# Moving the rounded operands of a float32r block kernel to other byte places in SBUF

## What is computed

```python
h = rms_norm(x, norm_pre_w)
proj = jnp.einsum('bsd,df->bsf', h, w_in)              # 1024 -> 10256
qkv_a, z_a, beta_a, dec_a, qkv_b, z_b, gate_logits = jnp.split(proj, cuts, axis=-1)
qkv_a = silu(causal_depthwise_conv(qkv_a, conv_w))      # then l2_normalize of q and k
oa = gated_delta_rule(qa, ka, va, g, beta)              # chunks of 64, 8 heads
ya = rms_norm(oa, dn_onorm_w) * silu(z_a)
ob = moba_attention(qb, kb, vb, rel_bias)
yb = ob * silu(z_b)
merged = gates[:, :, 0] * (ya @ w_branch[0]) + gates[:, :, 1] * (yb @ w_branch[1])
out = x + rms_norm(merged @ w_out, norm_post_w)
```

## Time and profile before

| | |
|---|---|
| median of 3 runs | 357.52 us (357.3 to 357.66) |
| the profiled execution | 357.55 us |
| its span, first to last instruction | 355.8 us |
| PE busy | 347.6 us, 98% |
| PEld (weight loads) busy | 318.4 us, 89% |
| DVE, ACT, POOL busy | 270.0, 218.8, 58.7 us |
| granted TensorE clock, mean | 0.998 |

### The profile page before, as it was taken

The page is one execution under the profiler, slowest core; times in us unless marked ns, Lnnn a source line. Parts: engine busy times, 40 slices in busy tenths (PEclk is TensorE's granted clock), DMA queues, the critical chain, the costliest instruction groups (busy, mean ns, idle before and its releaser), DMA issues.

```text
span 355.8 us, 6674 instructions
## 1 busy us (share of the span) xinstructions
PE 347.6 (98%) x2387; PEld 318.4 (89%) x2387; DVE 270.0 (76%) x551; ACT 218.8 (62%) x483; POOL 58.7 (16%) x114
## 2 busy tenths in 40 slices
PE   7999999999999999999999999999999999999993
PEld 5889998888899999999999999999998888888882
DVE  3869897599997868978788797878977656566744
ACT  5877894542457667686867766777676544425421
POOL 1534436500050000301103020030301101000011
PEclk9999999999999999999999999999999999999999
DMA  8667948793698485446745565465534735766423
GB/s 264 178 193 194 334 158 270 198 329 119 167 257 228 121 214 141 121 122 164 188 120 128 145 178 147 120 164 145 165 121 138 247 118 172 254 226 236 124 113 118
DMA packets 76206, 63.48 MB, mean 178 GB/s; under 512 B 4724, under 2 KB 62478, under 8 KB 76174
## 3 DMA queue, kind: packets, MB, share of 16 engines
q1 hardware_dynamic: 73838, 59.37, 57.3%
q0 software_dynamic: 1152, 3.30, 3.1%
q10 hardware_dynamic: 1184, 0.39, 0.5%
HBM read 61.46 MB, written 1.59 MB: 177 GB/s over the span
## 4 chain that ended last, share of the span: by engine, by line
PE 84%; DVE 8%; DMA 3%; issue 2%; ACT 1%; POOL 0%; DVEq 0%; SPq 0%; ACTq 0%; POOLq 0%
PE banks L1395 40%; PE banks L1450 15%; PE banks L1657 6%; PE banks L1413 6%; DVE w_lo L919 3%; DVE sub L1061 2%; DMA xin<-in_x_dram 1%; DMA raw<-in_w_in_dram 1%; DMA sub<-m_blocks 1%; PE banks L1545 1%; PE banks L1523 1%; PE banks L1562 1%; PE banks L1551 1%; PE banks L1380 1%; DVE sub L1063 1%
## 5 line engine op out<-in xcount | busy, mean ns | idle before, releaser
L919 DVE TENSOR_TENSOR w_lo<-raw,w_hi 128x1024 fp32r<-128x1024 f32 x102 | 123.8, 1220 | 42.3 <-ACT w_hi L670 41.6
L670 ACT CAST w_hi<-raw 128x1024 fp32r<-128x1024 f32 x103 | 107.2, 1047 | 30.0 <-PE banks L1450 12.3
L1395 PE MATMUL banks<-h_hi,w_hi 128*128 128x256 f32 x440 | 64.0, 288 | 0.2 <-DVE acc L989 0.2
L1395 PE MATMUL banks<-h_lo,w_hi 128*128 128x256 f32 x440 | 59.4, 277 | 0.0
L1395 PE MATMUL banks<-h_hi,w_lo 128*128 128x256 f32 x440 | 59.3, 277 | 0.0
L1395 PEld LDWEIGHTS banks<-h_hi,w_hi 128*128 128x128 f32 x440 | 55.2, 189 | 0.7 <-DVE acc L989 0.3
L1395 PEld LDWEIGHTS banks<-h_hi,w_lo 128*128 128x128 f32 x440 | 54.2, 188 | 0.0
L1395 PEld LDWEIGHTS banks<-h_lo,w_hi 128*128 128x128 f32 x440 | 54.2, 188 | 0.0
L989 DVE SCALAR_TENSOR_TENSOR acc<-banks,vec,acc 128x255 f32<-128x255 f32 (+2 forms) x72 | 34.5, 480 | 3.7 <-ACT acc L790 1.5
L616 POOL TENSOR_TENSOR so<-so,rnq 128x2 f32<-128x2 f32 x8 | 2.0, 251 | 162.8 <-ACT junk L857 162.8
L790 ACT ACTIVATE acc<-banks,vec 128x256 f32<-128x256 f32 x16 | 7.6, 473 | 17.4 <-PE banks L1395 17.4
(11 more groups left out here) (258 smaller groups left out, 607.6 us busy)
## 6 DMA issues: line engine op xcount, KB each, us to landing
raw<-in_w_in_dram SPq DMA_DIRECT2D x80, 512.0 KB, 4.9
raw<-in_w_branch_dram SPq DMA_DIRECT2D x16, 512.0 KB, 4.7
raw<-in_w_out_dram SPq DMA_DIRECT2D x8, 512.0 KB, 4.2
xin<-in_x_dram SPq DMA_DIRECT2D x2, 512.0 KB, 3.8
th_E<-g_rows POOLq DMA_DIRECT2D x2, 512.0 KB, 7.2
bias<-bias_rows POOLq DMA_DIRECT2D x1, 1024.0 KB, 7.5
raw<-in_x_dram SPq DMA_DIRECT2D x2, 512.0 KB, 3.7
out_dram<-xin SPq DMA_DIRECT2D x4, 256.0 KB, 2.0
```

The lines of the kernel that those rows point to most:

```text
L670: nc.scalar.copy(w_hi[:, t % SLOTS, :], raw[:, t % SLOTS, :]).then_inc(s_hi, 1)
L919: v.tensor_tensor(w_lo[:, t % SLOTS, cols], raw[:, t % SLOTS, cols], w_hi[:, t % SLOTS, cols].bitcast(F32), ALU.subtract).then_inc(s_lo, 1)
L1395: last = mm(ps, w, r, start=part == 0 and k == 0, stop=part == 2 and k == KT - 1)
```

## The change

The declarations are put in another order. No instruction is added, removed or moved on any engine; operands have other addresses. Six small tensors, 1,984 bytes in all, now stand ahead of `raw`, three more and `h`, `y` follow the weights, and `xin` and the rest come after these.

| tensor | byte before | mod 2048 | mod 256 | byte after | mod 2048 | mod 256 |
|---|---|---|---|---|---|---|
| `raw` | 16512 | 128 | 128 | 18496 | 64 | 64 |
| `w_hi` | 32896 | 128 | 128 | 34880 | 64 | 64 |
| `w_lo` | 49280 | 128 | 128 | 51264 | 64 | 64 |
| `h_hi` | 77632 | 1856 | 64 | 67840 | 256 | 0 |
| `h_lo` | 85824 | 1856 | 64 | 76032 | 256 | 0 |
| `y_hi` | 193088 | 576 | 64 | 84224 | 256 | 0 |
| `y_lo` | 209472 | 576 | 64 | 100608 | 256 | 0 |
| `wbd2` | 76416 | 640 | 128 | 17280 | 896 | 128 |
| `xin` | 65664 | 128 | 128 | 116992 | 256 | 0 |
| `kT_all` | 108992 | 448 | 192 | 141824 | 512 | 0 |
| `act` | 121280 | 448 | 192 | 154112 | 512 | 0 |
| `bT` | 125376 | 448 | 192 | 158208 | 512 | 0 |
| `pt` | 189504 | 1088 | 64 | 222272 | 1088 | 64 |
| `vtok_all` | 161216 | 1472 | 192 | 194048 | 1536 | 0 |

Slices start at whole multiples of 512 bytes (128 columns), 1024 bytes (256 columns) or 2048 bytes (512 columns) behind the start of their tensor.

```diff
+        gt = sb("gt", [P, 12, NC, HEADS])
+        wbd2 = sb("wbd2", [P, KT, 4 * HEADS], F32R)
+        ssqk = sb("ssqk", [P, NC, HEADS])
+        ng = sb("ng", [P, NC, HEADS])
+        so = sb("so", [P, 8])
+        mx = sb("mx", [P, 8])
         raw = sb("raw", [P, SLOTS, D])
         w_hi = sb("w_hi", [P, SLOTS, D], F32R)
         w_lo = sb("w_lo", [P, SLOTS, D], F32R)
+        bd = sb("bd", [P, NC, 2 * HEADS])
+        alog = sb("alog", [P, HEADS])
+        dtb = sb("dtb", [P, HEADS])
+        h_hi = sb("h_hi", [P, KT, SEQ], F32R)
+        h_lo = sb("h_lo", [P, KT, SEQ], F32R)
+        y_hi = sb("y_hi", [P, 2, HEADS, SEQ], F32R)
+        y_lo = sb("y_lo", [P, 2, HEADS, SEQ], F32R)
         xin = sb("xin", [P, NC, D])
...
         wbd = sb("wbd", [P, KT, 2 * HEADS])
-        wbd2 = sb("wbd2", [P, KT, 4 * HEADS], F32R)
         bd_lo = sb("bd_lo", [P, NC, 2 * HEADS])
-        alog = sb("alog", [P, HEADS])
-        dtb = sb("dtb", [P, HEADS])
-        h_hi = sb("h_hi", [P, KT, SEQ], F32R)
-        h_lo = sb("h_lo", [P, KT, SEQ], F32R)
...
-        y_hi = sb("y_hi", [P, 2, HEADS, SEQ], F32R)
-        y_lo = sb("y_lo", [P, 2, HEADS, SEQ], F32R)
```

More of the change, by code:

```diff
@@ L140, in build @@
         wbd = sb("wbd", [P, KT, 2 * HEADS])
-        wbd2 = sb("wbd2", [P, KT, 4 * HEADS], F32R)
         bd_lo = sb("bd_lo", [P, NC, 2 * HEADS])
-        alog = sb("alog", [P, HEADS])
-        dtb = sb("dtb", [P, HEADS])
-        h_hi = sb("h_hi", [P, KT, SEQ], F32R)
-        h_lo = sb("h_lo", [P, KT, SEQ], F32R)
         bias = sb("bias", [P, HEADS, SEQ])
         tiny = sb("tiny", [P, 32])
-        bd = sb("bd", [P, NC, 2 * HEADS])
-        gt = sb("gt", [P, 12, NC, HEADS])
         tab = sb("tab", [P, 11, HEADS])
-        ng = sb("ng", [P, NC, HEADS])
         grow = sb("grow", [HEADS, SEQ])
-        ssqk = sb("ssqk", [P, NC, HEADS])
         tk = sb("tk", [P, 2, NC, HEADS])
@@ L178, in build @@
         junk = sb("junk", [P, 512])
-        so = sb("so", [P, 8])
         lac = sb("lac", [P, 2, 2, P])
         sc = sb("sc", [P, BIAS_W])
-        mx = sb("mx", [P, 8])
         pt = sb("pt", [P, BIAS_W])
         y32 = sb("y32", [P, 2, SEQ])
-        y_hi = sb("y_hi", [P, 2, HEADS, SEQ], F32R)
-        y_lo = sb("y_lo", [P, 2, HEADS, SEQ], F32R)
         m0 = sub[:, 0:D]
```

## The result

The changed kernel takes 359.64 us (median of 4, 359.44 to 360.07) where the kernel before takes 357.54: a ratio of 1.0061, 95% interval 1.0044 to 1.0079. It is slower by 2.1 us. The forecast was "no visible effect", 357.5 us; the range held the time, the direction was wrong.

What follows compares the result with a forecast made beforehand. PE was taken as the bound, at full clock. All terms were 0, so the span stayed 355.8 + 0 us and the median forecast was 357.5 us, no visible effect (chance 0.42); range 353.5 to 360.0 us.

Steps and rivals of the forecast that it cites:

- What bounds the kernel: PE, busy 347.6 of 355.8 us and 84% of the chain; four lines with rounded operands alone are 67%.
- Step (a) and (b): Rounded matmuls on PE: new places of the weights (`raw`, `w`) and of `h`, `y` change their time by 0.
- Step (c): All other tensors moving, including `xin`, the VectorE `w_lo` step and float32 matmuls: 0, with 0.2 us either side before PE.
- Float32 matmuls of the heads: Float32 matmuls on PE, whose operands also move: 0, because row pairs at different places took equal time.
- Rival 3: L1395's 1320 weight loads at odd multiples of 64 bytes make PE wait; mostly 358.3 to 360 us; chance 0.24.
- rival 2: Rounded matmuls at L1395 and the 512-column lines lose much of their surplus; 347.8 to 355 us; chance 0.12.
- Rival 1: 512-column lines run faster with moving weights at `h`'s old place modulo 256; 1.0 us, giving 356.5 us; chance 0.22.
- Rival 4: Whole kernel: the declarations don't set the tensors' places; would give 357.5 us as well; no separate chance.
- The terms beside PE: First transfer `xin`, 4.34 us, and VectorE's `w_lo` step, 1218 ns each: 0 with 0.2 us on either side.

Runs made afterwards that it cites:

- `all_shift`: The kernel before with every tensor moved together by 1984 bytes, all distances between tensors kept; 357.45 us, ratio 0.9993.
- `cst_act_place`: The kernel before with `cst` and `act`, both operands of the transposes L1537 and L1540, at the change's distances from `h` and `w`; 358.04 us, ratio 1.0019.
- `rest_place`: The changed kernel with `w`, `h` and `y` put back to their old places modulo 256, everything else as in the change; 359.43 us, ratio 1.0048.

## Why the prediction was wrong

**What bounds the kernel** held: PE was the bound, and what the stretches lost, 2.2 us, came through in the span, which grew by 2.4.

**Step (a) and (b), the places of `w` and `h`: 0.** Right, and for the reason given last: the distance is unchanged. `all_shift` gave `w`, `h` and `y` the change's places modulo 256 and moved all others with them: 0.9993. But the reason given first, that no pair of rows sees its place, was wrong. The rows compared operands at one distance modulo 256 only; the same places at another distance cost 6 us. That the distance modulo 512 doesn't count was right (229.0 against 229.2 ns at 64 and 320, and at L1395 the fast rate at 320 before and at 64 in `cst_act_place`). So was it that crossing 2 KB costs nothing: every second slice of `h` crosses, and the single starts go 113, 113, 114 by turns of three.

**Step (c), everything else: 0.** This is the step that failed: "Float32 matmuls of the heads: 0". `rest_place`, in which only the other tensors differ from before modulo 256, has 25 slow stretches and 359.43 us. I asked whether a moved float32 matmul would itself take longer, and it does not: L1545 to L1552 take what they took. I did not ask what it does to the rounded stretch behind it. The row for this stood in the trace: two rates for identical stretches, 2.74 and 2.83 us. I used it as a price and left open what chooses between them. Two of 46 were slow, and the other 44 were fast because of places that the change did not keep. By what mechanism those places act on the stretch behind stays open.

**Rival 3** had the direction and, per matmul, the price: 3.8 ns. Its cause was wrong. Weight loads at an odd multiple of 64 bytes cost nothing (`all_shift`), and "all of them at that rate" became 24 more stretches, 576 matmuls, 2.2 us. Its sign, L1395 above 115 ns with the 512-column lines unchanged, came true in 26 of 46 stretches: the sign fitted a second cause as well. That the range held the time is luck; all 44 fast stretches at the slow rate would have been 4.0 us, 361.5 us. The slack of 1 ns that it reckoned with, and the floor of 112.5 ns in rival 2, are misread: the transposes at L1556 to L1558 have a load each and come every 110 ns, so a load does not need 112.5. **Rival 1** fell: with `w` moving at 64 modulo 256, the 72 matmuls take 16.50 us in `all_shift` and 16.51 in the changed kernel. Its observation, that 512 columns carry more than twice the surplus of 256, belongs to the distance: at distance 0 it is 227.1 ns. **Rival 2** fell too: no place or distance tried brought L1395 below 113.3 ns. **Rival 4** fell: the declarations set the places, as the table has them, and moving single ones moved the time by up to 1.6%.

**The terms beside PE** were 0 as taken: `xin` 4.35 us against 4.34, and the `w_lo` step 1218 ns in both.

## What to carry to other kernels

Before moving tensors in a kernel of float32r matmuls, write down the distance of every moving operand to its stationary one modulo 256, and keep it; it was worth 1.6% here, and the profile of one kernel need not show it, since here it was the same, 64, in all rows. When identical groups of instructions show two durations, ask at once what selects them: the change that looks neutral may be one that turns the selector. A bisection of allocations has to hold all distances modulo 256 but one, which pads in front and behind do.

## What was not expected of the hardware

- A float32r matmul's time in a dense stream depends on where its two operands stand to each other modulo 256 bytes, `w` less `h` or `y` here. With 256 moving columns (`w` stationary) it is 113.3 ns at 64 and 117 to 120 ns at 0, 32, 96, 128, 192 and 224; with 512 columns (`w` moving) 227.1 ns at 0, 229.2 at 64, 232.5 at 128 and 233.3 to 233.5 at 32, 96, 192 and 224.
- At distance 64 the stream runs at one of two rates, 113.3 and 117.7 ns, and keeps the one it takes in its first matmuls to the end of the 24; at 96, 192 and 224 there is more than one rate too; the granted clock is 0.998 to 0.999 in the spans of both kernels.
- Places of operands of the float32 matmuls between the stretches, whose own time doesn't change, can select that rate: 2 slow stretches of 46 before, 10 with `cst` alone moved, 25 in `rest_place`. How is not known.
